# Prompt attention: the scores of two coming jobs issued together, ahead of a pair's turns

## The chip, the cores and the metric

The kernel runs on one core of a Trainium2 chip. The metric is the device time of one execution in microseconds (us); the time of a version is the median of its runs. Five engines work side by side and are kept in order by semaphores: TensorE (PE in the profile, PEld its weight loads), VectorE (DVE), ScalarE (ACT), GpSimd (POOL) and SyncE (SP), which here issues DMAs. Each engine runs its own instructions strictly in the order of issue (only weight loads may run ahead of products).

## The reference

The reference is one layer of a decoder for two groups of requests, a prompt of 1024 tokens and 8 single decode tokens. The part that matters is the attention of the prompt. A query block of 128 tokens has three branches, and for each head each branch is scores, a softmax with a linear distance penalty, and a product with the values; the three results are scaled by gates and added:

```
def query_block(c):
    ...
    o_c, p_c = compressed_branch(qb, pos_q, kv_cmp, slopes)      # 64 compressed blocks of keys
    idx, valid = select_blocks(p_c, pos_q, n_sel)
    o_s = selected_branch(qb, pos_q, kv_g, idx, valid, slopes)   # with 1024 tokens: all keys up to the query
    o_w = window_branch(qb, pos_q, kv_wb, pos_k, slopes)         # the last 512 keys
    return gate_branches(gb, o_c, o_s, o_w)                      # sigmoid gates times the three, added
```

There are 8 heads of 64 channels and 2 groups of keys. After it come decode attention, a gated recurrence, a merge and an MLP, which the change does not touch.

## The kernel before

The prompt's attention is cut into 128 jobs. `job(j)` (L346) gives head, query block and branch: the head pair is j // 32, the query block i is j // 4 mod 8, j // 2 mod 2 tells the selected branch (0) from the window branch together with the compressed one (1), and j mod 2 is the head of the pair. So four jobs make a quad: both heads' selected jobs, then both heads' window jobs of one query block. A job of block i has i + 1 blocks of 128 keys in the selected branch, and up to five and the 64 compressed keys in the window branch. `groups(j)` splits them into a first group of up to four and a second of the rest.

Each job goes through these steps, each on one engine, in one hand-written order:

- `scores(j)` on PE (L1188): products (L1225, L1227, L1233, L1234, L1240, L1241) and added masks (L1229, L1235, L1242) into PSUM banks 0 to 3. A job takes one bank or two (`banks`, L369): two for the selected jobs of blocks 4 to 7 and the window jobs of blocks 3 to 7. `held_by(j)` (L381) is the last earlier job whose banks it takes over, and `scores` waits until the exponentials of that job are done (L1207). `scored(j)` (L385) is the last job whose scores can be issued once the jobs up to j have had their exponentials.
- `maxima(j)` on DVE (L2407): the row maxima (L2416, L2422), straight from PSUM.
- `exp(j)` on ACT (L1897): the exponentials out of PSUM into the probabilities, with their sums (L1909 for the selected branch, L1915 for the window and compressed ones, each followed by a short read of the sum).
- `turn(j, gi)` on PE (L1246): transposes (L1259) of a group of blocks into PSUM bank 4 or 5, in alternation.
- the copy of the first group by ACT (L1941) and of the second by DVE, `second(j)` (L2445, L2454).
- `pv(n)` on PE (L1262): the products with the values (L1279) of the jobs 2n and 2n + 1, into bank 6 or 7. It waits for both jobs' copies.

Once in a quad the output is finished: ACT copies the output parts (`parts`, L1923), PE turns them (`turn_parts`, L1288), DVE scales them and adds the three branches (`scaled_sum`, L2440 and L2442), PE turns the sum (`turn_sum`, L1293), and ACT copies it (`out`, L1928).

The order on PE is the loop at L1296: all scores that fit go first; then step j issues the scores from `scored(j - 1) + 1` to `scored(j)`, the turns of job j, in even steps j the value products of the jobs j - 2 and j - 1, in steps with j = 2 mod 4 the output turns of the quad before, and in the next step the turned sum. DVE (L2458) and ACT (L1931) have loops of their own. In step j, DVE does the maxima of the same scores as PE's step, then the second group's copy of job j, then in steps with j = 2 mod 4 the scaled sum. ACT does in step j the exponentials of the jobs `scored(j - 2) + 1` to `scored(j - 1)`, so for jobs of two banks that of job j + 1, then the copy of job j's first group; then in steps with j = 1 mod 4 the copy of the output parts. In some steps ACT and DVE also prepare queries and keys for later heads (L1857, L1861, L2359 to L2374).

Of the kernel before, what the change touches and what calls it, by code (L numbers as in the profile page):

```python
# [164 lines left out]
def hybrid_step(nc, x_p, x_s, c_cmp, c_sel, c_win, state, table, w_in, cmp_w, cmp_pos, lb_logits, norm_g,  # L165
                w_br_a, w_br_b, w_out, ln1_g, ln1_b, w_up, w_down, ln2_g, ln2_b, consts, kpos, dbias, before_d,
                y_p, y_s_out, cmp_p, sel_p, win_p, hg_p, cmp_s, sel_s, win_s, hg_s):
    with ExitStack() as ctx:
# [174 lines left out]
        NJ = 16 * NQ  # L343
# [15 lines left out]
        def groups(j):  # L359
            bl = blocks(j)  # L360
            return [bl[:4]] + ([bl[4:]] if len(bl) > 4 else [])
# [19 lines left out]
        def held_by(j):  # L381

            return max((x for x in range(j) if bank_at[x] + 4 < bank_at[j + 1]), default=-1)

        def scored(j):  # L385

            return max(x for x in range(NJ) if held_by(x) <= j)
# [3 lines left out]
        def evacuations(gr):  # L391

            full = sum(n == P for _, _, n, _ in gr)
            return [(P, 0, P * full)] * (full > 0) + [(NCMP_P, P * full, P * (full + 1))] * (full < len(gr))
# [237 lines left out]
        def copied(i):  # L632

            mine = wsteps[i][1] in BY_ACT
            return (w_act if mine else w_dve), sum((s in BY_ACT) == mine for _, s in wsteps[:i + 1])
# [51 lines left out]
        def part_high(x, ci):  # L687

            _, k0, k1, tile, at = BRANCH_PARTS[x]
            c0, cn = CHUNKS[ci]  # L690
            return tile[:, at:at + k1 - k0, c0:c0 + cn]
# [395 lines left out]
        def _(pe):  # L1087
# [158 lines left out]
            def turn(j, gi):  # L1246

                h, i, wc = job(j)
                if gi == 0:
                    pe.wait_ge(e_act, exps(j))  # L1250
                turned = first_group[j] + gi
                if turned >= 2:
                    before_j, before_gi = turned_by[turned - 2]
                    if before_gi:
                        pe.wait_ge(t_dve, second_groups[before_j + 1])
                    else:
                        pe.wait_ge(t_act, before_j + 1)
                for b, (br, k0, n, col) in enumerate(groups(j)[gi]):
                    mm = pe.transpose(PS[0:n, 4 + turned % 2, P * b:P * (b + 1)], probs(j, col, n), ident)  # L1259
                mm.then_inc(t_ps, 1)  # L1260

            def pv(n):  # L1262

                h, i, wc = job(2 * n)
                g, j1 = h // 4, 2 * n + 1
                pe.wait_ge(t_act, j1 + 1)
                pe.wait_ge(t_dve, second_groups[j1 + 1])
                if wc == 0 and n >= 4:
                    pe.wait_ge(o_act, 2 * (n // 2 - 1))
                bl = blocks(2 * n)  # L1270
                for b, (br, k0, r, col) in enumerate(bl):
                    if br == 2:
                        v = vcN[:, g, :]
                    else:
                        at = P * br + HD * g
                        v = kvV[:, k0 // P, at:at + HD]
                    for two in range(2):
                        c = P * ((br + 1) % 3)
                        mm = pe.matmul(PS[HD * two:HD * (two + 1), 6 + i % 2, c:c + P], v[0:r, :],  # L1279
                                       PT[(2 * n + two) % 3][0:r, b // 4, P * (b % 4):P * (b % 4 + 1)],  # L1280
                                       start=(wc == 0 and b == 0), stop=(br == 2 or b == len(bl) - 1 - wc),
                                       skip_group_check=True)
                mm.then_inc(pv_ps, 1)

            def turn_parts(n):
                pe.wait_ge(o_act, 2 * n + 1)
                for a in range(3):
                    mm = pe.transpose(PS[:, 6 + n % 2, P * a:P * (a + 1)], out_parts(n)[:, P * a:P * (a + 1)], ident)  # L1288
                mm.then_inc(ot_ps, 1)

            def turn_sum(n):
                pe.wait_ge(os_dve, 2 * n + 2)
                pe.transpose(PS[:, 6 + n % 2, 3 * P:4 * P], out_sum(n), ident).then_inc(ot_ps, 1)  # L1293
# [2 lines left out]
            for x in range(scored(-1) + 1):  # L1296
                scores(x)
            for j in range(NJ + 1):
                if j < NJ:
                    for x in range(scored(j - 1) + 1, scored(j) + 1):  # L1300
                        scores(x)
                if j < NJ:
                    for gi in range(len(groups(j))):
                        turn(j, gi)
                if j >= 2 and j % 2 == 0:
                    pv(j // 2 - 1)
                if j % 4 == 2 and j >= 6:
                    turn_parts(j // 4 - 1)
                if j % 4 == 3 and j >= 7:
                    turn_sum(j // 4 - 1)  # L1310
# [402 lines left out]
            for p, t in enumerate(LN_ORDER):  # L1713
# [21 lines left out]
                elif p == 1:  # L1735
# [4 lines left out]
                    for k in (0, 2, 7):  # L1740
                        for c in range(2 if k == 7 else 4):
                            j, half = c // 2, c % 2
# [1565 lines left out]
```

## Time and profile before

| | us |
|---|---|
| median of 3 runs | 2046.31 |
| lowest and highest run | 2040.78, 2050.05 |
| the profiled execution, its own time | 2041.56 |
| its span in the profile | 2039.7 |
| around the span (the difference) | 1.9 |

| engine | busy us | share of the span |
|---|---|---|
| PE | 2000.0 | 98% |
| DVE | 1284.8 | 63% |
| ACT | 742.8 | 36% |
| POOL | 314.5 | 15% |

The busy time of PE is modelled at its ends, so a wait shorter than a product's own tail does not show as idle time. What a wait costs is read better from the starts of the instructions in the timeline, which is in order of time and gives the start, the duration, the engine, the line and what the instruction reads and writes.

### The profile page before, as it was taken

Reading aid. Unit: us, or ns where it says so; the run is one execution under the profiler, and the core shown is the slowest. Engines: PE = TensorE matmul, PEld = TensorE weight load, DVE = VectorE, ACT = ScalarE, POOL = GpSimd, SP = SyncE. Lnnn points to the kernel's source line nnn. Section 1 sums busy time; section 2 is a strip of 40 time slices with the busy share of each in tenths; the row PEclk is TensorE's granted clock in tenths of the full one; section 3 lists DMA queues with packets and bytes.
Section 4 is the critical chain, followed back from the end, with each engine's and each line's share of the span. In section 5 each row is a group of like instructions: output and inputs, shape, how many; then the busy total and the mean of one; then the engine's idle time right before and its main releaser. Section 6 shows DMA issues by size and latency. Waiting matters only on the chain.

```text
span 2039.7 us, 35913 instructions
## 1 busy us (share of the span) xinstructions
PE 2000.0 (98%) x14826; PEld 1763.5 (86%) x14826; DVE 1284.8 (63%) x2214; ACT 742.8 (36%) x1432; POOL 314.5 (15%) x405
## 2 busy tenths in 40 slices
PE   8999999999989999999999999999999999999998
PEld 8997777769769999999999986898888888888896
DVE  3127777656642566766422327768888888888867
ACT  3127878754422454545211112132222322222323
POOL 0012000001320222321000000011132211121206
PEclk9999999999999999999999999999999999999999
DMA  9423010227662222323112213121111211111112
GB/s 221 128 68 130 12 43 12 94 106 259 221 229 52 59 59 49 74 49 106 42 32 63 73 51 116 32 83 42 44 50 48 67 42 42 45 50 49 55 42 84
DMA packets 140750, 159.21 MB, mean 78 GB/s; under 512 B 25842, under 2 KB 122443, under 8 KB 135724
## 3 DMA queue, kind: packets, MB, share of 16 engines
q1 hardware_dynamic: 132556, 114.14, 18.6%
q0 software_dynamic: 8032, 42.78, 6.7%
q8 instruction: 118, 1.93, 0.4%
q14 instruction: 44, 0.36, 0.1%
HBM read 141.32 MB, written 19.76 MB: 79 GB/s over the span
## 4 chain that ended last, share of the span: by engine, by line
PE 88%; DVE 6%; ACT 2%; SPq 1%; issue 1%; DMA 1%; POOL 0%; DVEq 0%; ACTq 0%; POOLq 0%
PE PS L1025 52%; PE PS L1801 12%; PE PS L1279 4%; PE PS L1367 3%; PE PS L1259 3%; PE PS L1696 2%; PE PS L1225 1%; PE PS L1352 1%; DVE arena L3021 1%; PE PS L1227 1%; PE PS L1605 1%; PE PS L1787 1%; PE PS L1288 1%; SPq L897 1%; PE PS L1480 1%
## 5 line engine op out<-in xcount | busy, mean ns | idle before, releaser
L1025 PE MATMUL PS<-x_low,w_high_mlp 128*128 128x344 f32 x1056 | 337.7, 320 | 0.0
L3021 DVE TENSOR_TENSOR arena<-arena,PS 128x512 f32<-128x512 f32 x336 | 225.1, 687 | 96.4 <-PE PS L1801 89.6
L1025 PE MATMUL PS<-x_high,w_low 128*128 128x344 f32 x768 | 246.0, 320 | 0.0
L1025 PE MATMUL PS<-x_high,w_high_mlp 128*128 128x344 f32 x720 | 231.3, 321 | 0.0
L1025 PEld LDWEIGHTS PS<-x_low,w_high_mlp 128*128 128x128 f32 x1056 | 198.3, 188 | 3.1
L1025 PE MATMUL PS<-x_low,w_high_hgrn 128*128 128x344 f32 x600 | 191.9, 320 | 0.0
L2169 ACT ACTIVATE aT<-PS 128x344 f32<-128x344 f32 x90 | 41.0, 456 | 373.2 <-PE PS L1025 314.3
L1801 PE MATMUL PS<-w_down_parts_high,hidden_parts_high 128*128 128x512 f32 x392 | 155.8, 397 | 1.1
L1801 PE MATMUL PS<-w_down_parts_high,hidden_parts_low 128*128 128x512 f32 x392 | 154.3, 394 | 0.0
L1025 PE MATMUL PS<-x_high_a,w_low 128*128 128x344 f32 x480 | 153.4, 320 | 0.0
L1025 PE MATMUL PS<-x_high_b,w_low 128*128 128x344 f32 x468 | 149.6, 320 | 0.0
L1025 PEld LDWEIGHTS PS<-x_high,w_high_mlp 128*128 128x128 f32 x720 | 135.4, 188 | 15.3 <-issue 12.9
L1025 PEld LDWEIGHTS PS<-x_high,w_low 128*128 128x128 f32 x768 | 144.2, 188 | 0.0
L3261 POOL TENSOR_TENSOR arena<-arena 128x128 f32<-128x128 f32 x42 | 19.7, 468 | 756.3 <-DVE arena L2942 756.3
L1847 ACT ACTIVATE arena<-PS 128x344 f32<-128x344 f32 (+1 forms) x105 | 47.0, 457 | 227.6 <-PE PS L1025 227.4
L1049 DVE TENSOR_TENSOR w_low<-wring,w_high_mlp 128x1024 fp32r<-128x1024 f32 x44 | 53.8, 1225 | 104.7 <-ACT w_high_mlp L1043 104.7
L1025 PEld LDWEIGHTS PS<-x_low,w_high_hgrn 128*128 128x128 f32 x600 | 112.9, 188 | 0.0
L1025 PE MATMUL PS<-x_high_a,w_high_hgrn 128*128 128x344 f32 x300 | 98.0, 327 | 0.3 <-issue 0.3
L2422 DVE TENSOR_REDUCE arena<-PS 128x1 f32<-128x640 f32 (+7 forms) x128 | 89.3, 702 | 12.8 <-PE PS L1229 11.9
L1025 PE MATMUL PS<-x_high_b,w_high_hgrn 128*128 128x344 f32 x300 | 97.3, 324 | 0.0
L1043 ACT ACTIVATE w_high_mlp<-wring 128x1024 fp32r<-128x1024 f32 x44 | 46.1, 1050 | 130.2 <-DMA wring<-in_w_in 108.9
L1801 PEld LDWEIGHTS PS<-w_down_parts_high,hidden_parts_high 128*128 128x128 f32 x392 | 73.6, 188 | 21.9 <-DVE arena L3021 7.0
(495 smaller groups left out, 4934.2 us busy)
## 6 DMA issues: line engine op xcount, KB each, us to landing
wring<-in_w_in SPq DMA_DIRECT2D x100, 256.0 KB, 3.4
wring<-in_w_up SPq DMA_DIRECT2D x64, 256.0 KB, 3.2
arena<-in_w_down SPq DMA_DIRECT2D x16, 1024.0 KB, 4.9
arena<-in_x_prompt SPq DMA_DIRECT2D x16, 512.0 KB, 3.9
x_high_kept<-x_high_att SPq DMA_DIRECT2D x1, 4128.0 KB, 14.4
arena<-in_w_out SPq DMA_DIRECT2D x2, 2048.0 KB, 8.5
out<-in_cache_win_kv SPq DMA_DIRECT2D x1, 4088.0 KB
out<-arena SPq DMA_DIRECT2D x7, 512.0 KB
```

The lines of the kernel that those rows point to most:

```text
L1025: mm = pe.matmul(out, w, x, start=(start and k == 0 and i == 0), stop=(stop and k == tiles - 1 and i == 2))
L1043: act.activation(dst[:, :, 0:m], wring[:, n % WR, :, 0:m], ACT.Copy).then_inc(wh_act, 1)
L1049: dve.tensor_tensor(wl[:, n % WR, :, 0:m], wring[:, n % WR, :, 0:m], high[:, :, 0:m].bitcast(F32), ALU.subtract).then_inc(wl_dve, 1)
L1259: mm = pe.transpose(PS[0:n, 4 + turned % 2, P * b:P * (b + 1)], probs(j, col, n), ident)
L1279: mm = pe.matmul(PS[HD * two:HD * (two + 1), 6 + i % 2, c:c + P], v[0:r, :], PT[(2 * n + two) % 3][0:r, b // 4, P * (b % 4):P * (b % 4 + 1 ...
L1367: mm = pe.matmul(PS[:, 4 + 2 * (b % 2) + c, 0:256], cw2[:, c, 4 * half + q, :], xt2[:, n % 2, 256 * (4 * c + q):256 * (4 * c + q + 1)], st ...
L1696: mm = pe.matmul(out, wring[:, n % WR, 4 * ab + k, :], a[:, k, c0:c0 + cn], start=(k == 0), stop=(k == 3))
L1801: mm = pe.matmul(PS[:, 5 + d % 3, :], h, w, start=(first and i == 0), stop=(i == 2), skip_group_check=True)
L1847: act.activation(dst[0:m, c0:c0 + cn], unit_out(3 * n + ci, m, cn), fn).then_inc(u_act, 1)
L2169: act.activation(dst[:, i % 2, c0:c0 + cn], PS[:, (y + 2) % 4, 0:cn], ACT.Relu).then_inc(relu_act, 1)
L2422: dve.tensor_reduce(nm[:, 0:1], sc[:, 0:n], AX.X, ALU.max, negate=True).then_inc(m_dve, 1)
L3021: ins = dve.tensor_tensor(y, y, sums, ALU.subtract if m == 4 else ALU.add)
```

## The change

Only PE's order in the loop of the attention changes. In an even step the scores up to `scored(j + 1)` are issued, instead of those up to `scored(j)`; in an odd step none. The scores that stood ahead of the turns of job j + 1 so stand ahead of the turns of job j. The turns, the value products, the output turns and the turned sum keep their places in the steps. The orders of DVE, ACT, POOL and SP are as before, and so is every semaphore's value.

```diff
             for x in range(scored(-1) + 1):
                 scores(x)
             for j in range(NJ + 1):
-                if j < NJ:
-                    for x in range(scored(j - 1) + 1, scored(j) + 1):
+                if j < NJ and j % 2 == 0:
+                    for x in range(scored(j - 1) + 1, scored(j + 1) + 1):
                         scores(x)
                 if j < NJ:
                     for gi in range(len(groups(j))):
```

## Rows read from the trace of the kernel before

**Rows 1.** Busy time: stretch; its us, PE, PEld, DVE, ACT, POOL; PEclk, DMA, GB/s.

```profile
166.00:444.00 278.00, 268.43 (x2580) 208.77 (x2579) 191.48 (x488) 209.11 (x632) 4.96 (x5) 1.00 0.13 48
```

**Rows 2.** Waits of PE from 166 to 444 us: total, times, longest.

```profile
PE PS L1279 <- ACT arena L1941: 2.4, 3, 0.8
PE PS L1279 <- DVE arena L2454: 2.2, 3, 0.7
```

**Rows 3.** Timeline: start, us, engine, line, operation; jobs 57 to 60.

```profile
284.23 0.96 PE L1259 MATMUL PS<-consts_sb,arena 128*128 128x128 f32 x7
...
284.90 0.60 ACT L1941 ACTIVATE arena<-PS 128x512 f32<-128x512 f32 x1 [0.38 <-PE PS L1259]
...
286.04 0.82 PE L1259 MATMUL PS<-consts_sb,arena 128*128 128x128 f32 x6
...
286.73 0.22 ACT L1915 ACTIVATION_READ_ACCUMULATOR arena<-PS,arena 128x1 f32 x1
```

**Rows 4.** Timeline: turns of jobs 45 and 46, end of the exponentials of job 47.

```profile
255.27 0.64 PE L1259 MATMUL PS<-consts_sb,arena 128*128 128x128 f32 x4
...
256.46 0.72 PE L1259 MATMUL PS<-consts_sb,arena 128*128 128x128 f32 x5
...
257.66 0.22 ACT L1915 ACTIVATION_READ_ACCUMULATOR arena<-PS,arena 128x1 f32 x1
```

**Rows 5.** Timeline: from the value products ahead of an output turn to job 60's turns.

```profile
288.15 0.39 PE L1279 MATMUL PS<-arena 128*64 128x128 f32 x4
...
288.47 0.55 PE L1288 MATMUL PS<-consts_sb,arena 128*128 128x128 f32 x3
...
288.77 0.48 PE L1225 MATMUL PS<-k_high_twice,q_high_low 128*128 128x512 f32 x1
...
289.64 0.60 DVE L2442 TENSOR_REDUCE arena<-arena 128x128 f32<-128x384 f32 x1
...
289.85 0.82 PE L1259 MATMUL PS<-consts_sb,arena 128*128 128x128 f32 x6
290.15 1.22 DVE L2422 TENSOR_REDUCE arena<-PS 128x1 f32<-128x1024 f32 x1
...
290.51 0.27 PE L1293 MATMUL PS<-consts_sb,arena 128*128 128x128 f32 x1
...
291.56 1.07 PE L1259 MATMUL PS<-consts_sb,arena 128*128 128x128 f32 x8
...
292.42 0.19 ACT L1909 ACTIVATION_READ_ACCUMULATOR arena<-PS,arena 128x1 f32 x1
```

**Rows 6.** Timeline: output turns, job 127's turns and turned sum, no scores left.

```profile
436.61 0.55 PE L1288 MATMUL PS<-consts_sb,arena 128*128 128x128 f32 x3
...
436.99 0.82 PE L1259 MATMUL PS<-consts_sb,arena 128*128 128x128 f32 x6
...
438.43 0.33 PE L1293 MATMUL PS<-consts_sb,arena 128*128 128x128 f32 x1 [0.62 <-DVE arena L2442]
```

**Rows 7.** Timeline: the scores of job 39, from their start to the next turns.

```profile
238.04 0.36 PE L1225 MATMUL PS<-k_high_window,q_high_low 128*128 128x256 f32 x1
...
238.68 0.42 PE L1259 MATMUL PS<-consts_sb,arena 128*128 128x128 f32 x2
```

**Rows 8.** Timeline: output turns, turned sum, job 48's turns, end of job 49's exponentials.

```profile
258.13 0.55 PE L1288 MATMUL PS<-consts_sb,arena 128*128 128x128 f32 x3
...
259.95 0.33 PE L1293 MATMUL PS<-consts_sb,arena 128*128 128x128 f32 x1
...
261.05 0.74 PE L1259 MATMUL PS<-consts_sb,arena 128*128 128x128 f32 x5
...
261.35 0.19 ACT L1909 ACTIVATION_READ_ACCUMULATOR arena<-PS,arena 128x1 f32 x1
```

**Rows 9.** Busy time, columns as in group 1: the first and the last stretch.

```profile
0.00:20.00 20.00, 12.02 (x80) 11.30 (x80) 8.97 (x14) 9.66 (x16) 0.20 (x4) 1.00 0.77 241
...
2030.00:2039.00 9.00, 2.30 (x10) 1.51 (x8) 6.91 (x12) 1.15 (x3) 2.78 (x3) 0.83 0.44 175
```

## Prediction

> **What bounds the kernel now.** I looked first for the stretch the change can touch. The loop runs from the first scores product at 166 us to about 444 us, and in that stretch TensorE is busy for 268 of 278 us at the full granted clock, ACT for 209 and DVE for 191 [rows 1]. So TensorE sets the pace, and at most some 10 us of this stage are idle that a new order could win. The waits of TensorE say where a part of them lies: 4.6 us ahead of value products (L1279), for the copies of the turned probabilities on ACT and DVE [rows 2]. After that I read the timeline, to see how far ACT and DVE trail behind TensorE; the order of the instructions hides their chains, and the change alters just that order.
>
> **What the change does to the order.** Call S(x) the scores of job x, T(x) its turns, e(x) its exponentials on ACT, m(x) its maxima on DVE. For two-bank jobs the loop issued S(j+2), T(j), PV, then S(j+3), T(j+1). Now it issues S(j+2), S(j+3), T(j), PV, T(j+1). PV stays in the even step, so the products of the jobs before still stand between the two turns: what is joined is the scores only. Nothing is added, removed or resized: TensorE's work is the same, and no DMA, no SP and no POOL instruction moves. What moves is the scores of 66 jobs, and with them the wait of S(j+3) for e(j+1), which frees its banks: it now holds up T(j), PV and everything behind it on TensorE, and through T(j) the copies on ACT and DVE. ACT and DVE keep their own order. Three things follow, per head pair of 32 jobs (four such pairs, alike in period).
>
> **(a) The second scores of an even step that starts at j = 2 mod 4 wait for e(j+1) (window job), which ACT can start only after copying T(j-1).** At the quad of query block 6 the turns T(57) begin at 284.23, ACT's copy begins at 284.90, then come the copy of the output parts and e(59), whose last piece ends at 286.73 + 0.22 = 286.95: 2.72 us after the turns began. TensorE needs for these turns and for S(60), up to 286.04, only 1.81 [rows 3]. In the kernel before, T(58), PV and more stand there, so nobody waits. After, S(61) stands there and waits 0.91. At block 3 the same sum is 2.61 - 1.19 = 1.42 [rows 4]; the five of a head pair (blocks 3 to 7) lie between these, mean 1.21. The last has no scores behind it, so 19 of them: 23 us. ACT is itself sometimes late there, where it also stages queries; such a piece, about a copy's length of 0.60 [rows 3], stands ahead of T(j-1)'s copy at two blocks in each of three head pairs, so the bounds are 0 and 3.6 us; I take 2.
>
> **(b) The turned sum loses its cover.** Each quad turns its output parts (L1288), DVE scales and sums them (L2440, L2442), and TensorE turns the sum (L1293). Between the two, the kernel before issued S(j+3) and T(j+1), for j = 2 mod 4. The distance is 1.82 to 1.83 us in most quads of the trace (1.82 in [rows 8]), whatever stands between: at blocks up to 4 and at block 7 the DVE chain sets it; only in the steps of blocks 5 and 6 is TensorE's own work longer, at block 6 from 288.47 to 290.51, 2.04 [rows 5]. The trace even holds one quad as the change makes them all: the last one has no scores left, only T(127) between, and the distance is 436.61 to 438.43, 1.82, of which 0.62 idle [rows 6]. So the distance stays 1.82, and the scores product that was inside it is now paid outside: 0.64 for a small one [rows 7], 1.08 - (2.04 - 1.82) = 0.86 for the largest [rows 5]. The eight of a head pair lie between and add to 6.4; without the first (there is no earlier output) and the last, 30 of them: 24 us.
>
> **(c) The second scores of an even step with j = 0 mod 4 wait for e(j+1) (selected job), whose maximum DVE computes only behind that same scaled sum.** For block 7, from the start of the output turns at 288.47: the sum ends at 290.24, m(61) runs from 290.15 to 291.37, e(61) ends at 292.42 + 0.19 = 292.61, so 4.14 after the output turns [rows 5]. TensorE would reach S(63) after 1.82 plus the turned sum and S(62), 290.51 to 291.56, that is 2.87. Wait: 1.27. For block 4 it is 3.41 - 1.82 - 1.10 = 0.49 [rows 8]. Four a head pair (blocks 4 to 7 as the selected job), mean 0.87, 16 in all: 14 us. The time that a release takes from ACT to TensorE is not counted in the 35 waits of (a) and (c).
>
> **What it gives back.** PV waits in the kernel before because ACT and DVE have not copied the turns of job j-1 by then; now two scores stand between instead of one, some 0.4 to 0.9 us more, so the 4.6 us of [rows 2] mostly go. The bounds are 0 and all idle time of the stage, 10 us [rows 1]; I take 5. A change between kinds of products costs nothing that I count: before and after there is one step into PV and one out of it per two jobs; the turns after PV take the place of scores after PV, and the nearest row, the output turns behind PV at 288.47, starts before PV's modelled end, 288.15 + 0.39 [rows 5]. Price 0, bounds plus or minus 0.1 us for 64 steps.
>
> **The sum.** 23 + 2 + 24 + 14 - 5 = 58 us. The decode half starts where the loop ends, so the delay goes through in full. The profiled execution took 2041.6 us (span 2039.7 and 1.9 around it); after: 2041.6 + 58 = 2099.6. The median of the three runs, 2046.3, stands 4.7 above that execution, in a scatter from 2040.8 to 2050.1, so on the footing of the medians I say 2104. A difference of 0.5%, 10 us, is about what a measurement of this kernel can tell from no change.
>
> **The rivals.**
> 1. The exponentials are in time, only (b) binds. It needs ACT to be ready well under 1.8 us after the turns begin, where the trace has 2.61 to 2.72 [rows 3, 4]; against it speaks that ACT's order is unchanged and each piece has its row. It gives 24 - 5 = +19: 2065. Chance 0.08.
> 2. Not slower. The two scores in a row give ACT and DVE time to catch up, PV no longer waits, and (b) stays hidden because the displaced scores fall into time that was idle before. It decides at one point: if the displaced scores find idle time, since the stage has 10 us of it and (b) alone needs 24. At best: 2046 - 10 = 2036; with half of that, 2041. For it: the waits ahead of PV are real [rows 2]. Against: the distances of [rows 6]. Chance 0.05.
> 3. The clock. After the change TensorE is idle for about a fifth of the stage, in pieces of 0.5 to 1.5 us. In this trace the granted clock stays at full speed in the first 20 us, where TensorE is busy for only 12, and falls to 0.83 on average in the last 9 us, busy for 2.3 [rows 9]; of its two levels 1.2 and 2.4 GHz that is a mixture. A fifth of the stage's 268 us of work at the lower level would add 54: 2046 + 58 + 54 = 2158. The first row is much nearer to the stage after than the second: chance 0.04. On this the Trainium skill speaks against the change: "TensorE: Matmul & The Clock Gate", section "A second HAM failure mode: psum-queue depth-cycling", tells of a kernel whose TensorE idles briefly and often between groups of products while it cycles through PSUM banks, so that its clock swings between the levels. By that rule the sum would be that of this rival, by the row that of the forecast; the trace agrees with the rule only at its end.
> 4. The change does less than its words say: that the products come after both turns is not in the code, as told above; if the issue order were in effect the old one, 2046. The loop as printed speaks against it. Chance 0.02.
>
> **How the numbers follow.** The forecast has the rest, 0.81. Its own bounds: (a) 22 to 27, (b) 22 to 25, (c) 13 to 16, the gain 10 to 0, so 47 to 68 us on 2046, and 10 us on either side for scatter and for knock-on waits that I have not seen: 2083 to 2125. The range reaches down to rival 1: 2062 to 2125; above it lies rival 3, below it rivals 2 and 4. Faster by over 0.5% is half of rival 2, 0.03; within 0.5% the rest of it and rival 4, 0.04; slower 0.93.
>
> **What would show it.** In the profile after, TensorE's waits should name three things: scores (L1225) for exponentials (L1909, L1915), over 30 us; the turned sum (L1293) for L2442, some 15 to 25 us; and value products (L1279) hardly any more. The stage should last about 336 us instead of 278, all output-turn distances should be 1.82, and every later stage keep its length. I would be wrong if scores after an even step start without waiting (rival 1), if the stage gets shorter (rival 2), or if the granted clock in it falls (rival 3).

## The result and the profile after

The changed kernel takes 2105.31 us, median of 4 runs from 2103.31 to 2110.47; the kernel before, timed beside it, 2046.03 us, 4 runs from 2040.78 to 2050.05. The ratio is 1.0296 with an interval of 1.0275 to 1.0318: slower by about 3%. The profiled execution took 2103.31 us with a span of 2101.4, against 2041.6 and 2039.7 before: 61.7 us more.

All of it lies in the stage with the loop. The page's busy times of the changed kernel by engine:

```profile
PE 2012.2 (96%) x14826; PEld 1768.7 (84%) x14826; DVE 1286.4 (61%) x2214; ACT 746.5 (36%) x1432; POOL 319.0 (15%) x405
```

Its busy time by stretch, columns as in [rows 1]:

```profile
166.00:505.00 339.00, 280.63 (x2577) 213.75 (x2575) 192.82 (x488) 212.23 (x630) 5.10 (x6) 0.99 0.11 40
...
505.00:2101.40 1596.40, 1574.28 (x11133) 1405.66 (x11132) 1048.47 (x1632) 488.69 (x723) 295.38 (x368) 1.00 0.25 77
```

The instruction counts are what they were (TensorE 14826, DVE 2214, ACT 1432, POOL 405), and DVE and ACT are busy for 1.6 and 3.7 us more in the whole execution. Ahead of the loop little changed: the first scores start at 166.6 us, before at 166.1. The decode half has its old 1595.7 us within 0.7 us. The loop's stretch takes 339 us where [rows 1] has 278, and DVE and ACT are busy in it as long as before, within 3.1 us. TensorE idles 58.4 us there instead of 9.6. The remaining 12 us of the 61 are counted as busy: a product ahead of a wait counts to its own end, which the next product covers where one follows at once; and some products ran at half the clock (below).

TensorE's waits in that stretch (engine, line, what it waited for: us in total, times, longest), to be held against [rows 2]:

```profile
PE PS L1293 <- DVE arena L2442: 23.3, 31, 1.1
PE PS L1225 <- ACT arena L1915: 17.3, 17, 1.3
PE PS L1225 <- ACT arena L1909: 11.9, 16, 1.1
PE PS L1233 <- ACT arena L1915: 3.5, 3, 1.2
PE PS L1279 <- DVE arena L2454: 1.9, 3, 0.7
```

These are the three chains of the prediction, each in its own row. (a) is the second row with the fourth, which is the same wait where the scores begin on another line: 20 waits, 20.8 us (19 as counted, and one of 0.2 us at the start of the loop that the kernel before has too). (c) is the third: 16 waits, 11.9 us. (b) is the first: 31 waits, 23.3 us. In the kernel before the same row is small:

```profile
PE PS L1293 <- DVE arena L2442: 3.4, 8, 0.6
```

Of the 4.6 us ahead of value products 1.9 are left, all on DVE.

Now one place of each in the timeline of the changed kernel (start, us, engine, line, operation; in brackets the idle time and what ended it), first (a) at query block 6, the place of [rows 3], then (b) and (c) at block 7, the place of [rows 5]:

```profile
309.76 0.98 PE L1259 MATMUL PS<-consts_sb,arena 128*128 128x128 f32 x7
...
312.28 0.22 ACT L1915 ACTIVATION_READ_ACCUMULATOR arena<-PS,arena 128x1 f32 x1
...
312.56 0.50 PE L1225 MATMUL PS<-k_high_twice,q_high_low 128*128 128x512 f32 x1 [0.66 <-ACT arena L1915]
...
316.10 0.55 PE L1288 MATMUL PS<-consts_sb,arena 128*128 128x128 f32 x3
...
317.28 0.59 DVE L2442 TENSOR_REDUCE arena<-arena 128x128 f32<-128x384 f32 x1
317.79 1.21 DVE L2422 TENSOR_REDUCE arena<-PS 128x1 f32<-128x1024 f32 x1
317.93 0.33 PE L1293 MATMUL PS<-consts_sb,arena 128*128 128x128 f32 x1 [0.62 <-DVE arena L2442]
...
319.03 1.11 ACT L1909 ACTIVATE arena<-PS,arena 128x1024 f32<-128x1024 f32 x1 [1.32 <-DVE arena L2422]
...
320.29 0.50 PE L1225 MATMUL PS<-k_high_window,q_high_low 128*128 128x512 f32 x1 [1.10 <-ACT arena L1909]
```

The turns of job 57 start at 309.76, and S(61) at 312.56, 2.80 later; by [rows 3] the exponentials end 2.72 after the turns began. Here they end at 312.50, 2.74 after, and the product starts 0.06 later. The output turns of block 7 start at 316.10, and the turned sum at 317.93, 1.83 later, now with 0.62 us idle ahead of it, just as in [rows 6]. The maximum of job 61 stands behind L2442 on DVE, its exponential behind the maximum, and S(63) starts at 320.29, 4.19 after the output turns (4.14 by [rows 5]).

### The profile page after: what moved, and what is told of

Read it like the earlier page. It is cut to its first block, busy times and chain, and to the rows that moved or that the text cites. A ratio compares the mean times of both kernels' runs of the same rounds, so it can differ in the third digit from the quotient of the medians.

```text
span 2101.4 us, 35913 instructions
## 1 busy us (share of the span) xinstructions
PE 2012.2 (96%) x14826; PEld 1768.7 (84%) x14826; DVE 1286.4 (61%) x2214; ACT 746.5 (36%) x1432; POOL 319.0 (15%) x405
## 4 chain that ended last, share of the span: by engine, by line
PE 85%; DVE 7%; ACT 3%; issue 2%; SPq 1%; DMA 1%; POOL 0%; DVEq 0%; ACTq 0%; POOLq 0%
PE PS L1025 50%; PE PS L1801 12%; PE PS L1279 4%; PE PS L1367 3%; PE PS L1259 2%; PE PS L1696 2%; PE PS L1225 1%; PE PS L1352 1%; ACT arena L1915 1%; DVE arena L3021 1%; PE PS L1227 1%; DVE arena L2440 1%; DVE arena L2422 1%; PE PS L1605 1%; PE PS L1787 1%
## 5 line engine op out<-in xcount | busy, mean ns | idle before, releaser
L1025 PEld LDWEIGHTS PS<-x_high,w_high_mlp 128*128 128x128 f32 x720 | 135.4, 188 | 15.3 <-issue 12.9
L1941 ACT ACTIVATE arena<-PS 128x512 f32<-128x512 f32 (+4 forms) x152 | 69.8, 477 | 95.4 <-PE PS L1259 94.9
```

The source lines that it names most:

```text
L1025: mm = pe.matmul(out, w, x, start=(start and k == 0 and i == 0), stop=(stop and k == tiles - 1 and i == 2))
L1941: ins = act.activation(PT[j % 3][0:r, 0, c0:c1], PS[0:r, 4 + first_group[j] % 2, c0:c1], ACT.Copy)
```

## The experiments

The measure between all these kernels is the *stage*, the time from the first output turn (L1288) to the last: 265.8 us before, 327.6 after. A *quad* is the time from one output turn to the next. Eight of them make a head pair. In the kernels before and after they repeat from pair to pair to a few hundredths of a microsecond wherever the granted clock is 1.00 (the first pair lacks quads 1 and 2, and its quad 3 is shorter). So a quad of odd length, held against the granted clock in it, shows where the clock fell; "undisturbed" below is a quad at 1.00. In some of the kernels below a quad or two also differ between pairs at the full clock. Quads of the second head pair, in us; the last row is the sum of (a), (b) and (c) of the prediction, worked out for each quad in the same way, without the gain ahead of the value products:

| | 1 | 2 | 3 | 4 | 5 | 6 | 7 | 8 |
|---|---|---|---|---|---|---|---|---|
| before | 7.00 | 5.84 | 7.10 | 7.45 | 9.45 | 10.14 | 10.75 | 10.86 |
| after | 7.28 | 6.50 | 7.02 | 9.68 | 12.24 | 13.13 | 13.82 | 14.17 |
| difference | 0.28 | 0.66 | -0.08 | 2.23 | 2.79 | 2.99 | 3.07 | 3.31 |
| (a)+(b)+(c) | 0.84 | 0.64 | 0.66 | 2.28 | 2.59 | 2.76 | 2.76 | 3.39 |

**Half of the join.** From the kernel before, the scores are joined in one kind of even step only. Where the step starts at j = 0 mod 4, only chain (c) should bind; where it starts at j = 2 mod 4, (a) and (b).

```diff
-                if j < NJ:
-                    for x in range(scored(j - 1) + 1, scored(j) + 1):
+                if j < NJ and j % 4 != 1:
+                    for x in range(scored(j - 1) + 1, scored(j + (j % 4 == 0)) + 1):
```

> From the kernel before, the scores are joined only in the steps with j = 0 mod 4 (ahead of the turns of two selected jobs); the steps with j = 2 mod 4 are as before. Theory (three chains): only wait (c) can arise, scores for the exponentials whose maximum stands behind the scaled sum; the output turn to turned sum distances stay as before, so (c) is 0.49, 0.74, 0.88 and 1.05 us a head pair, 13 us in all, and some 2 us come back ahead of value products: about +11, 2057. Rival (every moved scores product has a price of its own on TensorE, whatever its step: 59 us over 66 jobs, 0.9 each): about half of the 59, so 2075.

Measured 2060.50 us (5 runs, 2056.41 to 2066.02), ratio 1.0073 (1.0040 to 1.0106). The stage is 281.2 us, 15.4 more than before, at the full clock throughout. That is more than the 11 expected and far from the rival's 30. The row of (c) stands in TensorE's waits as it does after, and that of (b) is the one of the kernel before:

```profile
PE PS L1225 <- ACT arena L1909: 12.2, 16, 1.2
PE PS L1293 <- DVE arena L2442: 3.4, 8, 0.6
```

The other half:

```diff
-                if j < NJ:
-                    for x in range(scored(j - 1) + 1, scored(j) + 1):
+                if j < NJ and j % 4 != 3:
+                    for x in range(scored(j - 1) + 1, scored(j + (j % 4 == 2)) + 1):
```

> From the kernel before, the scores are joined only in the steps with j = 2 mod 4 (ahead of the turns of two window jobs). Theory: waits (a), some 25 us, and (b), 24 us, arise in full, (c) does not, about 3 come back: +46, 2092. Rival of a price per moved product: about +30, 2075.

Measured 2094.06 us (4 runs, 2089.58 to 2104.86), ratio 1.0244 (1.0194 to 1.0293). Its waits are those of (b) and (a), and no wait for L1909 is left among them:

```profile
PE PS L1293 <- DVE arena L2442: 23.0, 31, 1.1
PE PS L1225 <- ACT arena L1915: 17.9, 17, 1.3
```

The stage of its profile is 320.8 us. Five quads in it are longer than their like in other pairs (11.31 and 11.30 for 9.72; 10.12, 10.52 and 7.38 for 7.62, 6.50 and 7.04), 10.0 us in all, with a granted clock between 0.50 and 0.94 in them. Without them the stage is 310.8, 45.0 more than before. So the halves cost 15.4 and 45.0, together 60.4, against 58.6 for both in one kernel (the stage after, without its own two disturbed quads): they add up within 2 us. The halves move 32 and 34 scores, so a price for each moved product, the rival, would have split about evenly. The split goes by which job is second.

**The maxima ahead of the sum.** On the changed kernel DVE computes the maxima of both joined scores in the even step, ahead of the scaled sum. That takes away what makes (c) late.

```diff
-                for x in range(scored(j - 1) + 1, scored(j) + 1):
-                    maxima(x)
+                if j % 2 == 0:
+                    for x in range(scored(j - 1) + 1, scored(j + 1) + 1):
+                        maxima(x)
```

> The changed kernel, and DVE computes the maxima of both joined scores in the even step too, ahead of the scaled sum; TensorE's order is that of the changed kernel. Theory: (c) goes, 14 us, since the exponentials of the selected job then wait only for ACT's copy; (a) and (b) stay: 2091. Rival of a price per moved product on TensorE: no change, 2105.

Measured 2087.33 us (4 runs, 2085.51 to 2098.43), ratio 1.0222 (1.0178 to 1.0267): 18 us of the change's loss are back. The stage is 309.0 us at the full clock; against 324.4, the stage after without its two disturbed quads, that is 15.4 us less, for the 14 of (c). Some 2 of them are not (c): quad 1 shrinks from 7.28 to 6.55, where the value products waited for DVE (1.9 us in the waits after), and that row is gone as well. The rows of (b) and (a) stay, that of (c) falls:

```profile
PE PS L1293 <- DVE arena L2442: 23.2, 31, 1.1
PE PS L1225 <- ACT arena L1915: 17.3, 17, 1.3
...
PE PS L1225 <- ACT arena L1909: 1.1, 3, 0.4
```

**The turned sum one step later.** On the changed kernel L1293 is moved behind the two scores of the next even step, so that TensorE need not wait for DVE's sum.

```diff
+                if j % 4 == 0 and j >= 8:
+                    turn_sum(j // 4 - 2)
                 if j < NJ:
                     for gi in range(len(groups(j))):
                         turn(j, gi)
...
-                if j % 4 == 3 and j >= 7:
-                    turn_sum(j // 4 - 1)
```

> The changed kernel, and the turned sum is issued after the next two scores, ahead of the next even step's turns. Theory: the idle time ahead of the turned sum goes everywhere, but where (c) follows (16 of 31 quads) the exponentials still end 3.4 to 4.1 us after the output turns, so there the scores wait by as much longer; only the other quads gain, 3.7 us a head pair: -14, 2091. If (b) and (c) were independent terms: -24, 2081. Rival of a price per moved product: no change, 2105.

Measured 2110.47 us (4 runs, 2105.54 to 2121.03), ratio 1.0311 (1.0270 to 1.0352). I was wrong by 20 us: no gain at all. The waits tell a part of why:

```profile
PE PS L1225 <- ACT arena L1909: 27.2, 16, 2.1
PE PS L1225 <- ACT arena L1915: 17.6, 18, 1.3
PE PS L1279 <- DVE arena L2454: 4.0, 3, 1.3
...
PE PS L1293 <- DVE arena L2442: 0.8, 2, 0.6
```

The 23.3 us of (b) are gone, but (c) has grown from 11.9 to 27.2. The second scores need e(j+1), whose maximum stands behind the same DVE sum. TensorE now arrives there sooner and waits the longer. (b) and (c) are two waits in a row on one DVE chain: taking the first away alone hands its time to the second. So much was expected. The miss lies elsewhere. In the first four quads of a pair, where (c) doesn't occur, only 1.4 us a pair are gained for the 3.7 expected: undisturbed they are 7.26, 5.60, 7.33 and 8.86 against 7.28, 6.50, 7.02 and 9.68. In quads 1 and 3 the wait moved on to the value products. The undisturbed quads 5 to 8 are each 0.1 longer, so at the full clock the stage would be some 321 us, 3 less than after. The stage of this profile, the slowest of the four runs, is 337.1, and the granted clock in it is 0.94: the clock took the other 16 us. The two fastest runs, 2105.54 and 2106.00, are level with the changed kernel.

**Both together.** If that reading holds, both edits in one kernel must win what neither the one nor the sum of their separate effects shows.

> The changed kernel with both edits, the maxima of both joined scores ahead of the scaled sum on DVE, and the turned sum issued after the next two scores. Theory: the turned sum no longer waits (23 us less than with the maxima alone, 2087); where selected scores follow, they now wait for ACT's chain of turns, copy and exponentials, about 0.65 us in 16 quads, +10; in the small quads some of the idle time moves to the value products, +3: 2077. If nothing but the place of the wait changes, as with the turned sum alone: 2087.

Measured 2077.94 us (4 runs, 2075.16 to 2084.32), ratio 1.0168 (1.0142 to 1.0194): 27 us below the changed kernel, where the maxima alone won 18 and the sum alone nothing. The stage is 300.9 us; two of its quads are 12.9 us long, for 11.3, at a granted clock of 0.87, and without them it is 297.8, 26.6 below the changed kernel's, where the two edits alone won 15.4 and some 3. What is left in the waits is (a), and 9.9 us ahead of the selected jobs' scores, for the 10 expected there:

```profile
PE PS L1225 <- ACT arena L1915: 17.2, 17, 1.3
PE PS L1225 <- ACT arena L1909: 9.9, 15, 1.3
```

**The exponentials first.** On the changed kernel ACT computes e(j+1) ahead of its copy of T(j-1), the cause that the prediction names for (a).

```diff
-                for x in range(scored(j - 2) + 1 if j else scored(-1), scored(j - 1) + 1):
-                    exp(x)
+                if j == 0 or j % 2:
+                    for x in range(scored(j - 2) + 1 if j else scored(-1), scored(j - (j == 0)) + 1):
+                        exp(x)
```

> The changed kernel, and ACT does the exponentials of job j+1 ahead of the copy of job j-1 (for even j), not behind it; TensorE and DVE are as in the changed kernel. Theory: (a) shrinks from about 1.2 to 0.5 us a wait, 19 of them, -13; (b) and (c) stay; in the small quads the copy now stands behind exponentials whose maximum is late, +5: 2097. Rival (ACT's order is no part of (a), the wait is for the turns and the exponentials alone): 2105.

Measured 2123.09 us (4 runs, 2116.98 to 2125.20), ratio 1.0371 (1.0344 to 1.0397): slower by 18 us, where a gain was expected. The same kernel was run once more, for a second trace:

> The changed kernel with the exponentials ahead of the copy, once more, for its trace. Its stage took 345.7 us, of which some 17 us are in quads that are longer than their like at a granted clock of 0.69 to 0.83. If these are falls of the clock: other quads, 0 to 17 us, the time between 2105 and 2125, while the quads at full clock are the same. If they belong to the order: the same quads.

It gave 2121.68 us and a stage of 343.0. Neither of the two readings holds alone. The quads at the full clock agree with the first profile's within 0.02 us, and some of the long quads stand elsewhere. But quads 1 and 2 of the second head pair are long both times (10.87 and 10.52, then 10.22 and 10.05, for 8.39 and 6.79), and so is the last quad 8 (15.38 and 15.20, at a clock of 0.89). All five runs of this kernel took 2117 to 2125 us, with a granted clock of 0.985 to 0.990 over the whole execution; the changed kernel has 0.993 to 0.997. So the falls come with this order, and only some of their places change. The waits of the first profile:

```profile
PE PS L1293 <- DVE arena L2443: 22.4, 31, 1.1
PE PS L1225 <- ACT arena L1909: 11.9, 16, 1.1
PE PS L1225 <- ACT arena L1915: 7.3, 17, 0.6
PE PS L1259 <- ACT arena L1942: 7.1, 4, 2.2
PE PS L1279 <- ACT arena L1942: 6.2, 12, 0.9
PE PS L1233 <- ACT arena L1915: 2.3, 3, 0.8
```

(a) does shrink, from 20.8 to 9.6. But 13.3 us of new waits stand against it, for the copy (L1942 here, L1941 before the edit). One of them in the timeline:

```profile
339.38 0.37 ACT L1915 ACTIVATE arena<-PS,arena 128x128 f32<-128x128 f32 x1 [3.16 <-DVE arena L2423]
...
340.67 0.59 ACT L1942 ACTIVATE arena<-PS 128x512 f32<-128x512 f32 x1
...
341.40 0.30 PE L1259 MATMUL PS<-consts_sb,arena 128*128 128x128 f32 x1 [1.63 <-ACT arena L1942]
```

For small jobs the maximum comes late, ACT stands idle 3.16 us for it, and the copy, which was ready to run, stands behind it; TensorE then waits for the copy's bank. The undisturbed small quads grow to 8.39, 6.80 and 8.34, 2.7 us a pair. In quad 4 the value products wait for the copy, which takes back what (a) gives there; quads 5 to 8 gain 2.1 us a pair. With undisturbed quads in place of the long ones (the last quad 8 left as it is) the stage comes to about 328, 4 above the changed kernel's 324.4. The other 17 us of its 345.7 are quads at a lower clock (below).

**All three edits,** to see whether (a) can be won once (b) and (c) are gone:

> The changed kernel with the joined maxima, the later turned sum and the exponentials ahead of the copy together. Theory: of the 59 us the chains of 10 (a), 7 (c) and a few us ahead of value products are left, since two-bank scores can't be released before the turns just ahead of them and the exponentials behind those: 2060, still slower than the kernel before. If the three edits take away all waits: 2040.

Measured 2073.57 us (4 runs, 2065.30 to 2076.81), ratio 1.0128 (1.0099 to 1.0157): 13.6 above what I expected. Its stage is 288.5 us, 22.7 more than before; the first output turn of the profiled execution came 10 us late besides, by a clock that fell ahead of the loop (below). The waits for (a) are down to 7.4, but the copy's waits came along:

```profile
PE PS L1225 <- ACT arena L1915: 7.4, 17, 0.6
PE PS L1259 <- ACT arena L1942: 5.7, 4, 2.2
PE PS L1279 <- ACT arena L1942: 4.6, 9, 0.9
```

So ACT's order was swapped for two-bank jobs only, where the maximum is in time, on top of the maxima and the sum:

```diff
-                for x in range(scored(j - 2) + 1 if j else scored(-1), scored(j - 1) + 1):
+                first = j % 2 == 1 and j + 1 < NJ and banks(j + 1) == 2
+                done = j % 2 == 0 and j > 0 and banks(j) == 2
+                for x in range(scored(j - 2 + done) + 1 if j else scored(-1), scored(j - 1 + first) + 1):
```

> As with all three edits together, but ACT's exponentials stand ahead of the copy only where the job has two banks. Theory: the quads of small blocks then lose the late copy that the exponentials of job j+1 cost there (7.2, 6.0 and 7.3 us a quad with all three, 6.0, 5.6 and 7.3 without ACT's edit), the large ones keep the shorter waits (10.3 to 12.3 against 11.3 to 13.4): 1.8 us a head pair off a stage of 288.5 us, so 281.5, about +16 over the kernel before: 2061. If the copy's place costs nothing in the small quads: no change from all three, 2065 to 2074.

Measured 2065.28 us (4 runs, 2060.56 to 2069.52), ratio 1.0091 (1.0056 to 1.0125). The stage is 282.2 us at the full clock. The small quads are back at 5.99, 5.60 and 7.29, and the large ones (10.32, 11.29, 11.95, 12.28) are those of all three edits. With the three chains cut, 42 of the 58.6 us that the join had added to the stage are won back (324.4 to 282.2). What remains against the kernel before lies mostly in quads 5 to 8, 4.6 us a pair; no kernel here beats the one before by more than its scatter.

**The turned sum later, without the join.** The kernel before with the edit of L1293 alone: if (b) is hidden there, nothing should change.

> The kernel before, only the turned sum is issued one step later, after the next scores and ahead of the next even step's turns. Theory: the idle time ahead of it in the quads of small blocks (some 6 us) goes, but part of it moves to the value products, whose copies on DVE stand behind the scaled sum: 2041 to 2044 against 2044, no change that can be told.

Measured 2041.91 us (12 runs, 2040.25 to 2050.27) beside 2045.34 for the kernel before (17 runs), ratio 0.9986 (0.9972 to 1.0000): no difference that this can tell. The stage is 264.5 us, 1.3 less. Quads 1 to 8 are 7.00, 5.53, 7.40, 7.45, 9.24, 10.10, 10.76 and 10.87; the second and the fifth are a little shorter, the third longer. The waits ahead of the turned sum, 3.4 us in the kernel before, fall to 0.6, and those of the value products for ACT grow from 2.4 to 3.8. That is what [rows 5] and [rows 8] say: without the join, other products fill the distance.

**The changed kernel again,** for the two long quads of its profile:

> The changed kernel once more, for its trace. Two of its 31 quads took 1.6 us longer than their like in other head pairs, where the granted clock was at 0.94 and 0.91 in the 20 us around. If these are falls of the clock: the same quads at full clock come out the same within 0.05 us, and the longer ones are others, in other places or another number. If they belong to the order of the work: the same two quads.

2105.66 us. Its two long quads are other ones: 15.37 and 15.40, where the others of their kind have 13.82, while the sixth quads of pairs 3 and 4, 14.77 and 14.73 in the first profile for 13.13, have 13.16 here. All other quads agree within 0.03 us. So which quads are long is no property of the order of work; that two are long in both executions, and none in the kernel before, may be.

## Why the prediction was right, point by point

**The bound.** That TensorE sets the pace and that its in-order stream carries the others' delays held throughout: every kernel's time followed the length of its stage, but for up to 10 us that the clock took ahead of the loop. From the last output turn to the end of the span it is 1597 to 1599 us in every profile.

**(a)** S(61) came 2.80 us after the turns, for 2.72 worked out. The profile shows 20.8 us of waits for the 23 predicted (and 2 more, see the sum); a wait counts only from the modelled end of the product ahead of it, so the rows are a little below the price. ACT's order as the cause was shown by the exponentials moved ahead: the wait fell by half. Why the other half stayed was not tried apart.

**(b)** The distance from output turn to turned sum is 1.82 to 1.83 us in all quads after; the last one, outside the pattern, has 2.00. The wait is 23.3 us for the 15 to 25 named, the price 24. The cover named in the prediction was the right one: without the join, moving the sum did nothing.

**(c)** 16 waits as counted, 11.9 us for 14. With the maxima ahead of the sum the row fell to 1.1, and the stage lost 15.4 us, some 2 of them in quad 1.

**The gain.** 4.6 us of waits fell to 1.9. I let both rows go, and the one on DVE stayed at 1.9 of 2.2. Quads 1 and 3 lie 0.56 and 0.74 us below the sum of the chains. In quad 3 the wait for ACT (0.81 us) is gone, as predicted. In quad 1 the value products start 3.59 us after the output turns before and 3.60 after: they still wait for DVE, and the work that (b) displaced runs within that time. So this part was saved in a way that I had not named. In the stage it comes to some 4 us, for 5 taken: the first head pair lacks quad 1, and its quad 3 had only 0.14 us of wait to lose.

**The sum.** 58 us predicted. The stage grew by 61.8. Two quads in it have 1.6 us each too much, where the clock fell; without them the growth is 58.6. By quads the chains come to 15.9 a full pair, less 1.3; measured were 15.25 (the first pair lacks quads 1 and 2 and the last has no scores left at its end, so the stage holds less than four times this). The difference of 0.65 a pair sits in quads 5 to 7. Most of it can be what the prediction left out by name, the release: in each of the 35 waits of (a) and (c) the product starts 0.05 us after ACT's last piece ends, 1.8 us in all and nine times in a full pair. The 2 us set aside for ACT's own lateness did not show: quads 6 and 7 of the last head pair, where ACT stages no queries, took 13.16 and 13.82 us in the second execution, those of the first pair, with staging, 13.14 and 13.82. The forecast of 2104 met a median of 2105.31. That it is this close is luck: the four runs spread over 7 us, and the 3.2 us of the clock stood in no term. That the two halves of the join, taken apart, cost 45.0 and 15.4 us of stage, where 46 and 11 were worked out from the same chains, is not.

**The rivals.** "Only (b) binds" fell with the waits for L1909 and L1915, 32.7 us together. "Not slower" fell at its own point: the displaced scores found idle time only in quad 1, and the quad of [rows 6] was indeed the pattern for all. "The order unchanged" fell with the timeline. "The clock" happened in small: 3.2 us, not 54. There my sign of a wrong forecast was too coarse. I wrote that a falling clock would refute it; the clock did fall, and the forecast held because of how little it fell.

**Where I was wrong behind the prediction.** For the sum moved later I priced the hand-over to (c), but not the next wait in the quads without (c): there the value products wait for copies that ACT and DVE had not made any sooner (1.33 us in quad 1 for 0.64 after, 0.86 in quad 3 for none). At the full clock that left 3 us of the 14 expected, and the clock took more (2091 expected, 2110.47 measured). For the exponentials moved first I priced -13 and +5. At the full clock quads 5 to 8 gave 2.1 us a pair, quad 4 nothing, and quads 1 to 3 cost 2.7; the clock, which I had not priced, took some 17 us (2097 expected, 2123.09 measured).

## What to carry to other kernels

Joining two products of one in-order engine moves the wait of the second in front of all that stood between them; price it by asking, on each other engine's queue, what must be finished before the second may start and how long after the last common event that is. Work that stands between a request and its answer is cover: look for a place in the old trace where the cover is missing already (the last turn of a loop), and read the price there. Waits on one chain don't add as savings: when one of two is taken away, see first whether the other only grows. And where an order makes an engine wait often, compare periods at the same granted clock before the total times are compared.

## What the runs showed of the hardware

**The clock falls in a stage full of short waits, here for a few microseconds, and in the next execution of the same kernel at other places.** Stretches of the changed kernel around one such fall (columns as in [rows 1]; the granted clock, third from the end of a row, is 1.00, 0.53 and 1.00):

```profile
459.00:462.80 3.80, 2.55 (x18) 1.60 (x15) 3.36 (x7) 1.59 (x3) 0.00 (x0) 1.00 0.00 0
462.80:466.40 3.60, 3.60 (x26) 3.12 (x27) 1.21 (x5) 1.68 (x6) 0.00 (x0) 0.53 0.00 0
466.40:470.00 3.60, 2.67 (x25) 1.94 (x22) 1.65 (x3) 2.17 (x8) 0.00 (x0) 1.00 0.00 0
```

The timeline of the changed kernel there, and ahead of it turns and value products of the same size in an earlier pair, at the full clock:

```profile
293.89 0.85 PE L1259 MATMUL PS<-consts_sb,arena 128*128 128x128 f32 x6
294.67 1.68 PE L1279 MATMUL PS<-arena 128*64 128x128 f32 x24
...
462.29 0.50 PE L1225 MATMUL PS<-k_high_window,q_high_low 128*128 128x512 f32 x1 [0.62 <-ACT arena L1909]
...
463.59 1.52 PE L1259 MATMUL PS<-consts_sb,arena 128*128 128x128 f32 x6
465.05 2.32 PE L1279 MATMUL PS<-arena 128*64 128x128 f32 x24
```

Just behind a stretch with 1.25 of 3.80 us idle, TensorE ran for 3.6 us almost wholly at 1.2 instead of 2.4 GHz: the turns took 1.52 us for 0.85. The quad lost 1.6 us. In the kernel before, the loop's stage ran at 1.00 [rows 1]. The Trainium skill, in "TensorE: Matmul & The Clock Gate", section "A second HAM failure mode: psum-queue depth-cycling", tells of something near it in another kernel: while the products cycle through PSUM banks, TensorE idles briefly between groups of them, and its clock swings between the two levels. The trace agrees with the direction; the cost here was 3.2 us in 328.

How much idle time there is doesn't decide it alone. The kernel with the maxima moved ahead was idle for 45 of 309 us in the stage and its clock stayed at 1.00; the exponentials moved first lost some 17 us. There the falls last longer, and some come back at the same place: quad 2 of the second head pair ran at 1.2 GHz from end to end in the first profile, 10.52 us for 6.79, and was 10.05 us long at a clock of 0.53 in the second. In the first profile the same three quads, 1 to 3, stand once at 0.72 and once, one head pair on, at 1.00 (the first two rows, stretches of 30 and 24 us that hold them; the third is quad 2 alone):

```profile
246.00:276.00 30.00, 24.84 (x161) 17.63 (x161) 14.46 (x42) 16.99 (x63) 0.00 (x0) 0.72 0.05 18
...
337.00:361.00 24.00, 18.36 (x166) 13.24 (x166) 13.66 (x41) 16.75 (x63) 0.00 (x0) 1.00 0.06 23
...
256.75:267.27 10.52, 9.67 (x49) 6.71 (x47) 4.69 (x13) 5.72 (x22) 0.00 (x0) 0.50 0.13 51
```

TensorE's work in the first two stretches takes 24.84 us and 18.36. What the longest idle pieces have to do with it, and why one pass falls and the other doesn't, these runs leave open.

**It falls where TensorE doesn't idle, too.** In the kernel before TensorE is busy without a gap from 60 to 80 us. Its clock falls at 76.6 us, just behind 64 products of one column each (L1148):

```profile
72.08 3.89 PE L1148 MATMUL PS<-arena 128*64 128x1 f32 x64
...
72.00:76.60 4.60, 4.60 (x69) 4.50 (x69) 1.62 (x3) 1.40 (x2) 0.00 (x0) 1.00 0.46 114
76.60:80.00 3.40, 3.40 (x14) 3.40 (x13) 0.62 (x3) 0.00 (x0) 0.00 (x0) 0.51 0.00 0
```

In all 13 profiles the clock falls at these products, from 2.0 us after the first of them starts to 1.4 us after the last ends. In three of them (the turned sum later, all three edits, the swap for two-bank jobs) a longer fall comes ahead of that one, in 128 products of 64 columns (L1139) that TensorE starts after 0.90 to 1.40 us of idle time (the changed kernel's first profile has 1.16 us there and no such fall). The row of that fall with all three edits:

```profile
59.00:72.70 13.70, 13.70 (x105) 13.58 (x102) 1.23 (x1) 1.44 (x2) 0.00 (x0) 0.50 0.85 278
```

Why it falls at these two places was not tried. In the last two of these profiles the loop's first output turn came some 10 and 9.5 us later than in the kernel before, though no instruction ahead of the loop had been changed. The executions of the kernel before scatter by as much (2040.8 to 2052.5 over all its runs), so the length of the stage tells these kernels apart better than their total times do.
